# Hybrid decoder layer: the output projection's head norms, and part of w_o's loading, carried out in the delta rule's block

## What is computed

```python
h = x + 0.5 * rms_norm(swiglu_ffn(rms_norm(x, norms[0]), f1_gu, f1_d), norms[1])
# the token mixer, of rms_norm(h, norms[2]) @ w_in
o_dn = gated_delta_rule(q_dn, k_dn, v_dn, g, beta, s0)       # 4 heads of 128, chunked, carries a state
o_dn = rms_norm(o_dn, dn_norm) * silu(z)                     # norm per head, gate z
o_sb = rms_norm(stick_breaking_attention(q_sb, k_all, v_all, past, sb_bias), sb_norm)   # 8 heads of 64
mixed = concatenate([o_dn, o_sb], axis=-1)
mix = mixed @ w_o                                            # 1024 x 1024
h = h + rms_norm(mix, norms[3])
h = h + 0.5 * rms_norm(swiglu_ffn(rms_norm(h, norms[4]), f2_gu, f2_d), norms[5])
```

## Time and profile before

| | before |
|---|---|
| three timed runs | 2700.06, 2714.72, 2715.28 us; median 2714.72 |
| profiled execution | 2705.19 us, of which the profile's span is 2703.3 us |
| mean granted TensorE clock | 0.97 |
| busy | TensorE 2507.6 us (93%), VectorE 1198.3 (44%), ScalarE 864.7 (32%), GpSimd 206.6 (8%) |
| DMA | 223.27 MB, mean 83 GB/s |

### The profile page before, as it was taken

One profiled execution on the slowest core, in us unless ns is written; L12 is line 12 of the kernel. 1 busy time (PEld: TensorE's weight loads), 2 busy tenths in 40 slices (PEclk: granted clock), 3 DMA queues, 4 the chain that ended last, 5 costly groups with the idle time before them and its releaser, 6 DMA issues. The chain is left out here.

```text
span 2703.3 us, 43422 instructions
## 1 busy us (share of the span) xinstructions
PE 2507.6 (93%) x18032; PEld 2217.0 (82%) x18032; DVE 1198.3 (44%) x1907; ACT 864.7 (32%) x1523; POOL 206.6 (8%) x170
## 2 busy tenths in 40 slices
PE   7999999999989988998968889599899999999996
PEld 7999999999969777787856755368899999999995
DVE  4433333333354365546336654557333333333335
ACT  5211111111134665556635454324311111111112
POOL 0000000000011111211120010022000000000003
PEclk9999999999999999999989999789899999999998
DMA  4111111111133121121166678423111111111112
GB/s 156 47 47 47 47 47 47 47 47 47 47 101 100 50 54 51 54 61 53 37 210 219 197 242 278 149 72 125 49 63 44 37 44 47 47 47 47 47 54 103
DMA packets 172899, 223.27 MB, mean 83 GB/s; under 512 B 12617, under 2 KB 120521, under 8 KB 172768
## 3 DMA queue, kind: packets, MB, share of 16 engines
q1 hardware_dynamic: 172768, 221.44, 25.3%
HBM read 190.69 MB, written 30.71 MB: 82 GB/s over the span
## 5 line engine op out<-in xcount | busy, mean ns | idle before, releaser
L649 PE MATMUL a_q<-a_uh,a_p_hi 128*128 128x352 f32 x672 | 244.4, 364 | 4.4 <-DVE a_ul L489 4.4
L650 PE MATMUL a_q<-a_ul,a_p_hi 128*128 128x352 f32 x672 | 221.2, 329 | 0.0
L651 PE MATMUL a_q<-a_uh,a_p_lo 128*128 128x352 f32 x672 | 221.1, 329 | 0.0
L183 PE MATMUL a_q<-a_uh,a_hi_g 128*128 128x352 f32 x528 | 171.8, 325 | 3.0 <-DVE a_lo_g L387 3.0
L183 PE MATMUL c_q<-c_uh,c_hi_g 128*128 128x352 f32 x528 | 171.3, 324 | 1.4 <-DVE c_ul L489 1.4
L183 PE MATMUL c_q<-c_uh,c_hi_u 128*128 128x352 f32 x528 | 170.6, 323 | 0.0
L183 PE MATMUL a_q<-a_uh,a_hi_u 128*128 128x352 f32 x528 | 170.6, 323 | 0.0
L184 PE MATMUL a_q<-a_ul,a_hi_g 128*128 128x352 f32 x528 | 170.5, 323 | 0.0
L185 PE MATMUL a_q<-a_uh,a_lo_g 128*128 128x352 f32 x528 | 170.3, 323 | 0.0
L184 PE MATMUL c_q<-c_ul,c_hi_g 128*128 128x352 f32 x528 | 169.9, 322 | 0.0
L185 PE MATMUL c_q<-c_uh,c_lo_g 128*128 128x352 f32 x528 | 169.7, 321 | 0.0
(11 more groups left out here) (467 smaller groups left out, 5837.0 us busy)
## 6 DMA issues: line engine op xcount, KB each, us to landing
b_page<-in_cache_k SPq DMA_DIRECT2D x128, 256.0 KB, 3.6
b_page<-in_cache_v SPq DMA_DIRECT2D x128, 256.0 KB, 3.9
a_p_raw<-in_w_in SPq DMA_DIRECT2D x28, 512.0 KB, 4.0
a_raw_g<-in_ffn_gu SPq DMA_DIRECT2D x11, 1024.0 KB, 5.1
a_raw_u<-in_ffn_gu SPq DMA_DIRECT2D x11, 1024.0 KB
a_raw_d<-in_ffn_d SPq DMA_DIRECT2D x11, 1024.0 KB, 4.9
c_raw_g<-in_ffn_gu SPq DMA_DIRECT2D x11, 1024.0 KB, 5.1
c_raw_u<-in_ffn_gu SPq DMA_DIRECT2D x11, 1024.0 KB
```

The source lines that it names most:

```text
L183: nc.tensor.matmul(out[:, 0:TB], wh, self.uh[:, c, cols], start=(c == 0), stop=False)
L649: nc.tensor.matmul(self.pm[at % 2][:, 0:TB], wh, self.uh[:, c, cols], start=(c == 0), stop=False)
L650: nc.tensor.matmul(self.pm[at % 2][:, 0:TB], wh, self.ul[:, c, cols], start=False, stop=False)
L651: mm = nc.tensor.matmul(self.pm[at % 2][:, 0:TB], wl, self.uh[:, c, cols], start=False, stop=(c == KC - 1))
```

## The change

1. **Head norms.** For tiles 0 to 6 (`EARLY_TILES` = 7) square, sums, scaling and gates are made in the delta rule's block, in new streams of SyncE (`head_gates`), ScalarE (`head_norms`) and VectorE (`finish`), at `begin(i)` + 18.5 to 20.8. The ScalarE square root and the reciprocal are replaced there by logarithm and exponential and one Newton step of three small VectorE operations. Only tiles 7 and 8 keep their head norms in the mix stage.
2. **w_o.** Rows 0 and 1 (`EARLY_ROWS`) are loaded in the delta rule's block to `w_early`. Rows 2 to 7 get buffers of their own, and are loaded at the mix stage's start without waits. The rounding is split into column halves (16 steps of 512 columns instead of 8 of 1024); the columns 0 to 511 of all rows come first.
3. **Room.** `Map` gets a `lead`, so that the first bytes of the feed-forward's map lie where `w_early` is; in the delta block `p5` becomes the same buffer as `p1`. As w_o's rows now lie in the buffers of the residual rows and of the middle norms' gains, those loads wait for the rounding (`w_lo` at `KC + 6` of 16).
4. **Due times.** The mix stage's streams and the sample's steps get other due times; the `PACE` table too.

The diff, without the changes of due times that are not spoken of:

```diff
...
-    def __init__(self, nc, tag, start, size):
-        self.nc, self.tag, self.start, self.size = nc, tag, start, size
...
-        assert offset + 4 * math.prod(shape[1:]) <= self.size, name
-        return self.nc.alloc_sbuf_tensor_at(f"{self.tag}_{name}", shape, dt, offset=self.start + offset)
+        end, (lead_at, lead) = offset + 4 * math.prod(shape[1:]), self.lead
+        assert end <= self.size and (end <= lead or offset >= lead), name
+        at = lead_at + offset if offset < lead else self.start + offset - lead
+        return self.nc.alloc_sbuf_tensor_at(f"{self.tag}_{name}", shape, dt, offset=at)
...
-        w_raw = [f_map.at(f"wo_raw{z}", 4096 * z, [P, D]) for z in range(3)]
+        w_raw = [w_early[:, k, :] for k in range(EARLY_ROWS)]
+        w_raw += [f_map.at(f"wo_raw{k}", o, [P, D])[:] for k, o in ((2, 98304), (3, 102400), (4, 57344), (5, 61440), (6, 8192), (7, 66560))]
...
+                for k in range(EARLY_ROWS, KC):
+                    yield -2.08 - 0.02 * k
+                    sp.dma_start(w_raw[k], w_o[k * P:(k + 1) * P, :]).then_inc(E(f"w_in{k}"), 16)
...
-                yield 0.32
+                yield -1.5
+                sp.dma_start(g_dn[:], dn_gain_row.partition_broadcast(P)).then_inc(E("gains_in"), 16)
+                sp.dma_start(g_sb[:], sb_gain_row.partition_broadcast(P)).then_inc(E("gains_in"), 16)
+                yield 0.25
+                sp.wait_ge(E("w_lo"), KC + 6)
+                load_h1(0)
+                load_h1(1)
...
             def first_weights():
-                yield 3.67
...
+                yield 3.56
+                sp.wait_ge(E("w_lo"), 2 * KC)
...
-                    yield i - 0.55
+                    yield i - 0.67 if i else -1.78
                     n = rows_of(i)
-                    pe.wait_ge(E("finished"), i + 1)
+                    at_least(pe, E("finished"), i + 1 - EARLY_TILES)
...
-                            yield i + 0.47 * half + 0.10 * k
+                            yield i + 0.49 * half + 0.10 * k
...
-                            if i == 0 and half == 0:
-                                pe.wait_ge(E("w_lo"), k + 1)
+                            if i == 0:
+                                pe.wait_ge(E("w_lo"), KC * half + k + 1)
...
-                for i in range(N):
-                    n = rows_of(i)
...
+                for i in range(EARLY_TILES, N):
+                    n, z = rows_of(i), i - EARLY_TILES
...
-                for k in range(KC):
-                    yield -1.22 + 0.31 * k if k < 2 else -0.64 + 0.09 * k
-                    act.wait_ge(E(f"w_in{k}"), 16)
...
+                for n in range(2 * KC):
+                    half, k = divmod(n, KC)
+                    yield -0.87 - 0.02 * n
+                    if half == 0 and k >= EARLY_ROWS:
+                        act.wait_ge(E(f"w_in{k}"), 16)
+                    cols = slice(half * 512, half * 512 + 512)
+                    nc.scalar.activation(w_hi[:, k, cols], w_raw[k][:, cols], ACT.Copy).then_inc(E("w_hi"), 1)
...
+                for n in range(2 * KC):
+                    half, k = divmod(n, KC)
+                    yield -1.13 + 0.06 * n
+                    dve.wait_ge(E("w_hi"), n + 1)
+                    cols = slice(half * 512, half * 512 + 512)
+                    nc.vector.tensor_tensor(w_lo[:, k, cols], w_raw[k][:, cols], w_hi[:, k, cols].bitcast(F32), ALU.subtract).then_inc(E("w_lo"), 1)
...
+EARLY_ROWS = 2
+EARLY_TILES = NT - 1
...
+        p1, p6 = s.sb("p1", [P, H, R]), s.sb("p6", [P, H, 2 * R])
+        p5 = p1
...
-            interleave(pages(), chunk_rows(), attended())
+            def head_gates():
...
+                for i in range(EARLY_TILES):
+                    yield begin(i) + 14
+                    at_least(sp, E("finished"), i)
+                    sp.dma_start(gate[:], gate_rows[i * P:(i + 1) * P, :]).then_inc(E("gate_rows_in"), 16)
+
+            def first_rows():
+                for k in range(EARLY_ROWS):
+                    yield begin(5) + 6.0 * k
+                    sp.dma_start(w_early[:, k, :], w_o[k * P:(k + 1) * P, :]).then_inc(E("w_early_in"), 16)
+
+            interleave(pages(), chunk_rows(), attended(), head_gates(), first_rows())
+            sp.wait_ge(E("w_early_in"), 16 * EARLY_ROWS)
...
+            def head_norms():
+                for i in range(EARLY_TILES):
+                    yield begin(i) + 18.5
...
+                    nc.scalar.activation(squares_h[:], mixed[:, i, :], ACT.Square).then_inc(E("squared_h"), 1)
+                    yield begin(i) + 19.5
+                    act.wait_ge(E("mean_h"), i + 1)
+                    nc.scalar.activation(root_h[:], mean_h[:], ACT.Ln).then_inc(E("log_h"), 1)
+                    act.wait_ge(E("log_h"), i + 1)
+                    nc.scalar.activation(root_h[:], root_h[:], ACT.Exp, scale=-0.5).then_inc(E("root_h"), 1)
...
+                for i in range(EARLY_TILES):
+                    yield begin(i) + 18.9
+                    dve.wait_ge(E("squared_h"), i + 1)
+                    for at_, w, h0, h1_ in heads_:
+                        nc.vector.tensor_reduce(mean_h[:, h0:h1_], squares_h[:, at_:at_ + DN].rearrange("p (h c) -> p h c", c=w),
+                                                AX.X, ALU.add).then_inc(E("reduced_h"), 1)
...
+                    for at_, w, h0, h1_ in heads_:
+                        step = nc.vector.tensor_scalar(mean_h[:, h0:h1_], mean_h[:, h0:h1_], 1.0 / w, EPS, ALU.mult, ALU.add)
+                    step.then_inc(E("mean_h"), 1)
+                    yield begin(i) + 19.3
...
+                    nc.vector.tensor_tensor(v, v, g_dn[:].rearrange("p (o c) -> p o c", o=1).broadcast_to([P, H_DN, P]), ALU.mult)
+                    yield begin(i) + 20.0
+                    dve.wait_ge(E("root_h"), i + 1)
+                    then(nc.vector.tensor_tensor(newton_h[:], root_h[:], root_h[:], ALU.mult))
+                    then(nc.vector.scalar_tensor_tensor(newton_h[:], mean_h[:], -0.5, newton_h[:], ALU.mult, ALU.mult))
+                    then(nc.vector.scalar_tensor_tensor(root_h[:], newton_h[:], 1.5, root_h[:], ALU.add, ALU.mult))
+                    nc.vector.tensor_tensor(a_heads(i), a_heads(i), r[:, 0:H_DN].broadcast_to([P, H_DN, P]), ALU.mult)
+                    nc.vector.tensor_tensor(b_heads(i), b_heads(i), r[:, H_DN:].broadcast_to([P, H_SB, DH]), ALU.mult).then_inc(E("scaled_h"), 1)
+                    yield begin(i) + 20.8
...
+                    nc.vector.tensor_tensor(a_heads(i), a_heads(i), v, ALU.mult)
+                    nc.vector.tensor_tensor(b_heads(i), b_heads(i), g_sb[:].rearrange("p (o c) -> p o c", o=1).broadcast_to([P, H_SB, DH]),
+                                            ALU.mult).then_inc(E("finished"), 1)
...
-    PACE = ((0, -1.20), (10, -0.54), (20, 0.37), (32, 1.19), (36, 1.54), (52, 3.36))
+    PACE = ((0, -0.85), (10, -0.63), (20, 0.37), (32, 0.29), (36, 1.54), (52, 3.36))
...
-        yield self.when(1.29)
+        yield self.when(3.77)
         sp.dma_start(self.qkv[:], self.qkv_nat[T_P:T, :]).then_inc(self.E("rows_in"), 16)
...
                    (qkv_nat, gate_nat, k_rows, v_rows, conv_rows, q_cols, k_cols), o_nat, ab, ident)
+        early_at = nc.sbuf_base + -nc.sbuf_base % 32
+        w_early = whole.sb("w_early", [P, EARLY_ROWS, D])
```

171 lines of the change are left out of this document (88 added, 83 removed).

## The result

The changed kernel takes 2729.64 us (median of 10 runs, 2721.79 to 2734.5), the kernel before 2713.89 us (10 runs, 2700.06 to 2717.38). The ratio is 1.007, with a 95% interval of 1.0052 to 1.0088: slower by 0.7%. I had forecast 2708 us in a range of 2688 to 2728. That it moved less than 1% was right; the number, its direction and the range were not.

The account below looks back on a forecast made before the run. TensorE was taken as the bound, nearly always busy in the feed-forward, with waits in the delta block and mix stage's lead-in. 2705.19 - 20 (mix stage) + 20 (delta block) = 2705; forecast 2708 us, range 2688 to 2728.

Parts of the forecast that it names:

- The tile's work stands before the third and the fourth step: Delta block: norms ahead of two steps of the chunk's inverse delay VectorE, and 2.6 us a tile reach TensorE.
- Tiles 3 to 5: Delta block, chunks with value rounds: 2.6 us a tile, 7.8 together; bounds 0 and 5.8 a tile.
- Tile 2: Delta block: its VectorE steps wait for GpSimd's 4.60 us product, which locks the shared ports; 5.7 us.
- Tiles 0 and 1: Delta block, chunks with key rounds: VectorE's waits between copies cover part of the work; 1.6 us each, 3.3 together.
- tile 6: Delta block's last chunk, a bare chain without page rounds: part of its 5.8 us fits in gaps; cost 3.4 us.
- the stage's gain is 11 + 9: Mix stage: tile 0 ends 11 us sooner, 9 us of waits leave tiles 1 and 2; 20 us, bounds 8 and 26.
- The lead-in: Mix stage's opening: first projection matmul at about 18.5 us instead of 31.0, first sample inverse at about 25.5.
- the second term: Mix stage, tiles 1 and 2: of their 43 us, 34 are TensorE's own need; 9 us of waits come off.
- the sign of being wrong: Prediction wrong if the mix stage shrinks by under 12 or over 27 us, or delta block grows under 8 or over 32.
- rival 2: Delta block pays in full, no gap recovered: 41 us, total 2730; slower once a tile costs over 2.9 us; chance 0.13.
- Rival 1: Delta block hides the work in VectorE's idle time: cost at most 5 us, total 2694; chance 0.24.
- Rival 3: Mix stage: w_o rows delay the sample rows, TensorE's order holds the projection; only 11 us won, total 2718; chance 0.15.

Follow-up runs that it names:

- experiment 1: Changed kernel without the head norms, gates and gate loads of tiles 0 to 6 (output not the reference's): 2698.22 us, ratio 0.9971 to the kernel before.
- experiment 5: Changed kernel with the same norms at later due times, ScalarE's logarithm and exponential behind its copy of u: 2706.8 us, ratio 0.9987 to the kernel before.
- experiment 7: Changed kernel with only tile 2's norms moved later, past GpSimd's product of 128x2080: 2719.22 us, ratio 1.0042 to the kernel before.
- experiment 3: Changed kernel with 100 extra 128x128 transposes on TensorE in the mix stage's lead-in: 2722.89 us, ratio 1.0051 to the kernel before.
- experiment 8: Changed kernel without the four 128x512 products that finish each of tiles 0 to 6: 2711.05 us, ratio 1.0009 to the kernel before.
- experiment 11: Changed kernel with the sample's 64 old-state products spread over tiles 0 to 1 (one PACE number): 2726.56 us, ratio 1.0065 to the kernel before.
- experiment 9: Kernel of experiment 5 plus the 100 lead-in transposes of experiment 3: 2705.72 us, ratio 1.0001 to the kernel before.
- experiment 10: Kernel before with 115 transposes of the identity on TensorE at the mix stage's opening: 2704.47 us, ratio 0.9998 to the kernel before.
- experiment 2: Kernel before with only the head norms and gates of tiles 0 to 6 moved into the delta block: 2730.43 us, ratio 1.0067.
- experiment 13: Changed kernel with later norms and spread old-state products, tile 6's head norms back in the mix stage: 2701.99 us, ratio 0.9967 to the kernel before.

## Why the prediction was wrong

The forecast was 20 us out of the mix stage and 20 us into the delta block. The profiles gave 9.4 out and 31.3 in.

1. **The block's price: the mechanism was right, but its size was not.** The cost is the wait for steps of the inverse, place by place as in "The tile's work stands before the third and the fourth step". In idle time of TensorE it came to 14.2 us, less than the 20 I had summed. What the sum did not hold at all, and this is the step that failed, is the other 17.1 us: the same matmuls on a lower granted clock (12.0 to 18.6 us in the other profiles of the same block). I had priced each delay at its own length, as if TensorE came back from a wait at full speed. The row for it was there, though in another stage: the earlier trace rows has the lead-in at 0.51 and the tiles behind it at 0.82. That the norms at this place bring the low clock is shown by experiments 1, 5 and 7: without the norms, or with them elsewhere, the block's low-clock time is 6.6 and 13.3 us, and moving tile 2 alone takes away the longest stretch. That they do it through TensorE's waits is argued, from what else could reach it; how long the low clock then lasts is not fixed by the waits (experiment 3).
2. **Tiles 3 to 5** were put at 2.6 us and cost 3.2 to 3.7. In experiment 3, where no half-clock stretch fell on tiles 4 and 5, they cost 2.2 and 2.1. The bound of 5.8 held.
3. **Tile 2** was put at 5.7 us and cost 11.4. The lock was foreseen, and VectorE and GpSimd met. I had placed the norms against the old timeline without the scan of 4.49 us right ahead of them, so the meeting fell on the third of the four products and not on the small steps. The stretch of 23.9 us at half speed, which begins in a wait ahead of the meeting, is in no term of mine. How the 11.4 us split between lock, scan and clock stays open; in experiment 8, without the four products and so without the meeting, tile 2 cost 3.3.
4. **Tiles 0 and 1** were put at 3.3 us together and cost 4.7; tile 6 was put at 3.4 and cost 4.8, of which part may be the last chunk's own clock.
5. **The mix stage: "the stage's gain is 11 + 9".** The lead-in was right to 1.3 us (first matmul at 17.2, inverse at 24.5). The step to tile 0 failed: I counted 32 small products at 6.0 us where 64 stand in the program (my description of the kernel has "some thirty" too), 56 of them in one run of 12 us, 13.7 us in all. So the first half's matmuls end 55.3 us after the opening, not at 46.5; the second half then takes its 6 us at full clock, as forecast. And the second term, 9 us of waits taken out of tiles 1 and 2, could not be had: by the earlier trace rows TensorE was busy 70.8 of the 75.6 us from the first matmul to tile 2, so 4.8 us was all the idle time there. The row that I cited for gaps bounded them, and I did not subtract. Tiles 1 and 2 did go from 43 to 35 us, but mostly because the samples' work had moved ahead of tile 0, which for that kept only 1.5 of its 11 us. So the stage shrank by 9.4 us, under the 12 that I had named as the sign of being wrong.
6. **The rivals.** The sign came out as rival 2 has it: it named 2.9 us a tile as the point of turning, and the tiles cost 4.5 on average. Its mechanism, with no gap recovered, would have cost 41 us in waits; the waits cost 14. So its number was nearly right for another reason. Rival 1 (hidden work) is refuted for this place, and nearly true for the place of experiment 5. Rival 3's 11 us in the stage were near the 9.4 measured. Its first half is refuted (the first projection matmul came at 17.2 us, so the sample rows were not to blame); its second, that TensorE's order holds the projection behind the sample's chain, came true for tile 0.
7. **The range** reached 2728 because I took 20 us as the likeliest price and never bounded the clock. With the clock's share of 17 us added to the block, my sum would have given 2709 - 20 + 37 = 2726, inside that range; with both measured terms it is 2709 - 9 + 31 = 2731, against 2729.6. So both terms had to be wrong to put the time outside.

On the clock, the Trainium skill, "TensorE: Matmul & The Clock Gate", section "What's actually happening", says that the low clock is the default and activity releases it. The trace bears out that waiting brings it. It does not bear out that any work lifts it: in the changed kernel the stage's clock stayed at 1.2 GHz for 38 us after the first projection matmul, with TensorE busy 33.7 of them (window 1769.3 to 1807.3 above).

## What to carry to other kernels

Before pricing waits that will be removed, subtract busy from window for the engine that bounds the stage: that difference is all that the waits themselves can give. More comes only with a higher clock for the same work, which here another order of products brought (experiment 11: 6.6 us of busy time), and filled idle time did not in any total that could be told from none (experiments 3, 9 and 10). When work is moved in front of an engine that feeds TensorE, price the wait twice, once for its length and once for the lower clock that the next work may run on; here the second was as large as the first (17.1 and 14.2 us). And try the same work at two or three other places in the fixed order before judging it: the same seven tiles' norms cost 31, 18 and 8 us by place alone.

## What the runs showed of the hardware

- TensorE's granted clock fell 2.5 us after TensorE's last matmul of the delta block in the kernel before (1714.3 and 1716.8 us) and 3.0 us after it in the changed kernel (1749.9 and 1752.9), where 8 transposes had begun at 1752.2. It came back 40 us after the work did in the changed kernel (1767.6 to 1807.5), and 3.6 us after the projection began in the kernel before (1747.4 to 1751.0), to fall again at 1754.4.
- The clock also fell with TensorE busy 3.0 of the 3.4 us since it had last risen (experiment 3, 1768.6 to 1772.0), behind products of 32x32 in part.
- The order of the same 676 matmuls changed how long it stayed low: with 56 products of 8 columns in one run it was low for 47.8 to 54.6 us of the stage (six profiles, stage 163.0 to 166.2 us), with them spread among products of 512 columns 41.0, 43.3 and, with one tile's norms less in the block, 34.1 us (stage 160.0, 160.4 and 156.8 us).
- The same block, with the same order, had 33.9, 47.8, 47.8 and 51.2 us of low clock in four profiles (experiment 3, the changed kernel, experiments 2 and 11) and took 252.8, 257.4, 257.4 and 257.5 us.
- VectorE's product of 128x512 beside GpSimd's of 128x2080 took 4.97 us instead of 0.69 and ended 0.5 us after it (1601.9 and 1601.4).
- The last chunk took 22.0 or some 27.3 us in different profiles, according to whether a stretch of 13.7 us at half clock fell on it, with unchanged code (experiments 10 and 13).
